# A two-layer transformer block on one core: 32 stored copies of a distance table in place of 128, and each later bias load split in four

## The reference

```python
d_own = pos[:, None] - (own * MOBA_BLOCK + blk_off)[None, :]
s_own = jnp.einsum('bhqd,bhkd->bhqk', qc, k_own) * scale
s_own = jnp.where(d_own >= 0, s_own + rel_table[:, rel_bucket(d_own)].astype(jnp.float32)[None], NEG)
p = jax.nn.softmax(logits, axis=-1)          # logits = s_own here
```

## Time and profile before

| | us |
|---|---|
| median of 3 runs | 2872.69 |
| lowest, highest of them | 2869.83, 2874.22 |
| the profiled execution, its own time | 2870.79 |
| its span (first to last instruction) | 2869.1 |

### The profile page before, as it was taken

One profiled execution on the slowest core, in us unless ns is written; L12 is line 12 of the kernel. 1 busy time (PEld: TensorE's weight loads), 2 busy tenths in 40 slices (PEclk: granted clock), 3 DMA queues, 4 the chain that ended last, 5 costly groups with the idle time before them and its releaser, 6 DMA issues.

```text
span 2869.1 us, 58709 instructions
## 1 busy us (share of the span) xinstructions
PE 2811.4 (98%) x22998; PEld 2767.3 (96%) x22998; DVE 1651.9 (58%) x2115; ACT 1251.6 (44%) x1531; POOL 114.2 (4%) x133
## 2 busy tenths in 40 slices
PE   7999999999999999999999999999999999999998
PEld 7888899999999999999999999999999999999998
DVE  6455677666666544554555755555655555555444
ACT  5345555444344344443444554444544444344333
POOL 0002220000000000000001400000000000000000
PEclk9999999999999999999999999999999999999999
DMA  6543455555555655556555445555555555555555
GB/s 218 125 131 105 111 145 169 187 174 196 183 183 175 197 185 178 188 182 185 174 175 166 160 156 184 186 184 184 176 177 190 190 185 185 185 177 190 184 170 176
DMA packets 141133, 499.99 MB, mean 174 GB/s; under 512 B 17405, under 2 KB 19837, under 8 KB 141024
## 3 DMA queue, kind: packets, MB, share of 16 engines
q1 hardware_dynamic: 136912, 491.36, 52.4%
q0 software_dynamic: 4112, 7.02, 1.7%
HBM read 494.06 MB, written 4.19 MB: 174 GB/s over the span
## 4 chain that ended last, share of the span: by engine, by line
PE 91%; DVE 3%; ACT 2%; DMA 1%; issue 1%; DVEq 1%; ACTq 0%; SPq 0%
PE acc L1199 29%; PE acc L1201 29%; PE acc L1200 29%; DVE wlo L744 1%; DMA raw<-in_wts 1%; ACT whi L424 1%; PE aux L1241 1%; PE aux L1232 0%; PE aux L1306 0%; PE aux L1308 0%; DMA h<-in_hT 0%; PE aux L1300 0%; DVE h L786 0%; PE aux L1421 0%; PE aux L1314 0%
## 5 line engine op out<-in xcount | busy, mean ns | idle before, releaser
L744 DVE TENSOR_TENSOR wlo<-raw,whi 128x1024 fp32r<-128x1024 f32 x926 | 1121.4, 1230 | 863.0 <-ACT whi L424 858.7
L1199 PE MATMUL acc<-xh,whi 128*128 128x256 f32 (+2 forms) x4976 | 1419.1, 285 | 26.4 <-DVE wlo L744 16.7
L1201 PE MATMUL acc<-xh,wlo 128*128 128x256 f32 (+2 forms) x4976 | 1404.9, 282 | 0.0
L1200 PE MATMUL acc<-xl,whi 128*128 128x256 f32 (+2 forms) x4976 | 1402.0, 282 | 0.0
L424 ACT ACTIVATE whi<-raw 128x1024 fp32r<-128x1024 f32 x926 | 954.4, 1054 | 868.4 <-PE acc L1201 790.5
L1199 PEld LDWEIGHTS acc<-xh,whi 128*128 128x128 f32 x4976 | 941.8, 189 | 37.1 <-issue 19.8
L1200 PEld LDWEIGHTS acc<-xl,whi 128*128 128x128 f32 x4976 | 938.9, 189 | 0.7
L1201 PEld LDWEIGHTS acc<-xh,wlo 128*128 128x128 f32 x4976 | 939.3, 189 | 0.0
L1199 PE MATMUL acc<-acth,whi 128*128 128x256 f32 x1408 | 396.8, 282 | 4.6 <-issue 4.5
L1200 PE MATMUL acc<-actl,whi 128*128 128x256 f32 x1408 | 396.3, 281 | 0.0
L1201 PE MATMUL acc<-acth,wlo 128*128 128x256 f32 x1408 | 396.2, 281 | 0.0
(11 more groups left out here) (281 smaller groups left out, 2370.7 us busy)
## 6 DMA issues: line engine op xcount, KB each, us to landing
raw<-in_wts SPq DMA_DIRECT2D x928, 512.0 KB, 4.3
h<-in_hT SPq DMA_DIRECT2D x4, 544.0 KB, 4.8
distances<-quads POOLq DMA_DIRECT2D x1, 2048.0 KB, 47.8
bias<-distances POOLq DMA_DIRECT2D x16, 128.0 KB, 2.4
out_T<-h SPq DMA_DIRECT2D x4, 512.0 KB, 3.5
bias<-in_rp POOLq DMA_DIRECT2D x16, 64.0 KB, 4.9
bias<-in_rp POOLq DMA_DIRECT2D x8, 44.0 KB, 4.6
bias<-in_rp POOLq DMA_DIRECT2D x8, 42.0 KB, 4.6
```

What stands on the lines that cost most here:

```text
L744: dve.tensor_tensor(wlo[:, slot_of(at, j), :], raw[:, slot_of(at, j), :], whi[:, slot_of(at, j), :].bitcast(F32), ALU.subtract).then_inc(l ...
L1199: pe.matmul(dst, hi, x_hi(kt), start=kt == 0, stop=False)
L1200: pe.matmul(dst, hi, x_lo(kt), start=False, stop=False)
L1201: last = pe.matmul(dst, lo, x_hi(kt), start=False, stop=kt == chunks * per_chunk - 1)
```

## The change

The stored table has 32 copies in place of 128. Row p of a group of 32 partitions reads copy p, and each 128-partition load becomes four loads of 32 partitions, whose start in the table is moved back by the group's first partition. DVE waits for the larger count of landed loads. The bias that arrives is the same.

```diff
+COPIES = 32
...
-    dist_dram = nc.dram_tensor("distances", (P, HEADS, DISTS + 1), F32, kind="Internal").ap()
+    dist_dram = nc.dram_tensor("distances", (COPIES, HEADS, DISTS + 1), F32, kind="Internal").ap()
...
+        MOBA_LOADS = 2 * (P // COPIES) * 16
...
-            pool.dma_start(dist_dram.rearrange("c h d -> h c d"), dist.unsqueeze(1).to_broadcast([HEADS, P, DISTS + 1]))\
+            pool.dma_start(dist_dram.rearrange("c h d -> h c d"), dist.unsqueeze(1).to_broadcast([HEADS, COPIES, DISTS + 1]))\
...
-                    pool.dma_start(bias2[:, t, :],
-                                   bass.AP(dist_dram.tensor, i * (DISTS + 1) + (SEQ - 1 - t * P),
-                                           [[HEADS * (DISTS + 1) - 1, P], [1, SEQ]])).then_inc(bias_landed, 16)
+                    for p in range(0, P, COPIES):
+                        pool.dma_start(bias2[p:p + COPIES, t, :],
+                                       bass.AP(dist_dram.tensor, i * (DISTS + 1) + (SEQ - 1 - t * P - p),
+                                               [[HEADS * (DISTS + 1) - 1, COPIES], [1, SEQ]])).then_inc(bias_landed, 16)
...
-                        scaled_scores(MOBA, i, bias2, (bias_landed, i * 32 + (16 * NA_DMAS * HEADS + 32)))
+                        scaled_scores(MOBA, i, bias2, (bias_landed, i * MOBA_LOADS + (16 * NA_DMAS * HEADS + MOBA_LOADS)))
```

## The result

| | before | after |
|---|---|---|
| median, us | 2872.44 (6 runs) | 2858.59 (6 runs) |
| lowest to highest | 2869.83 to 2874.22 | 2854.95 to 2860.08 |
| profiled execution's span | 2869.1 | 2858.4 |

The ratio is 0.995, with an interval of 0.994 to 0.996: 13.9 us faster by the medians. The two profiled executions differ by only 10.7 us.

A forecast was written before the change was run, and what follows sets the result against it. TensorE, busy 98% of the span, was taken as the bound, waiting only where the store delayed weight loads. 2870.79 - 14.69 = 2856.1 us, or 2858.0 by the runs' median; 2857.0 was predicted, half-way, range 2853.5 to 2865.

The forecast's parts named there:

- The store goes with its bytes: Table store on GpSimd's queue: a quarter of the bytes takes a quarter of 47.8 us, 12.0, ending near 113.7.
- The first weight load is in time: MLA head 0: the load issued behind the store at 104.53 lands by 117.0, before ScalarE rounds it near 117.9.
- The cover up to 121.9: MLA head 0: rounding the first chunk as late as 121.9 us costs TensorE nothing; the upper bound was 120.3.
- The whole excess goes, 14.69 us: MLA heads 0 and 1 fall from 68.21 us to twice undisturbed head 2, 53.52; everything behind moves forward 14.69 us.
- the forecast that the wait for `qkv` would be gone: MLA heads 0 and 1: a sign of success was that TensorE's waits for `pt` and `qkv` would be gone.
- The mask and the first NA bias earlier: GpSimd's mask load, small loads and addition move to about 115 to 126 us; price 0 to 1.95 us, taken as nothing.
- The eight loads: MOBA heads: eight bias loads for two, 4.5 us of GpSimd per head, hidden; cost nothing, upper bound 2 us.
- The rival of latency: Queue alternation, not backlog, delays the first load: only head 1 recovers, 7.3 us left, 2863.5 or 2865.4; chance 7%.
- The rival that the store was not the cause: The store is not the cause or its time does not follow its bytes: time stays 2870.8 to 2872.7; chance 4%.
- The Trainium skill's price: GpSimd DMA costs about 2.0 us plus bytes by 436 GB/s: store 6.8 us old, 3.2 new, so no gain, 2870.8.
- The rival of the serial loads: MOBA heads: eight small loads land one after another and slower than before; at 4.3 us each, about 2930; chance 3%.

The follow-up runs named there:

- copies64: Changed kernel with 64 copies stored and each bias load split in two: 2863.72 us, ratio 0.997 to the kernel before.
- two_copies: Kernel before with 2 copies stored, bias loads whole, rows read one element apart (wrong bias): 2857.26 us, ratio 0.995.
- split_only: 128 copies stored as in the kernel before, bias loads split in four as in the changed kernel: 2870.66 us against 2872.06, ratio 0.9999.
- store96: Kernel before with 96 copies stored, bias loads whole (wrong bias): one run, 2868.18 us.
- store_only: Kernel before with 32 copies stored, bias loads whole (wrong bias): 2859.98 us against 2872.06, ratio 0.9956.
- part128: Kernel before with its 2048 KB store read from 128 partitions of `h`, one 16 KB row each (wrong table): 2860.44 us, ratio 0.996.
- copies8: Changed kernel with 8 copies stored and each bias load split in sixteen, 32 loads a MOBA head: 2859.76 us, ratio 0.9963.

## Why the prediction was right

2857.0 was forecast, 2858.59 measured, and 13.85 us gained of 14.69. The forecast lay half-way between two sums, 2856.1 and 2858.0; the second, on the scale of the medians, is the nearer. Step by step:

- *The store goes with its bytes*, forecast 12.0 us: 12.5. Right, and the four points from 12.5 to 47.8 are nearly proportional.
- *The first weight load is in time*, forecast by 117.0: issued at 104.30, no load took over 10.9, so by 115.2. Right. The median of the loads there is 4.5 us, where I wrote near 3.5.
- *The cover up to 121.9.* Borne out by copies64: a rounding at 124.70 is late, and TensorE waits 4.1 us for `pt`. It comes 23.49 us into the head, against 23.87 before, where the wait was 4.5, so each us beyond the cover costs about one.
- *The whole excess goes, 14.69 us.* The mechanism is right, the term was too large by 0.8. "Heads 0 to 2 have the same six chunks and the same attention steps" was not like with like. A group of eight chunks ends in head 1 at step 1 (`j % CD == CD - 1` for j = 7), and TensorE waits there 1.5 us for the eviction, also when the store is nearly nothing (two_copies). That this boundary is the reason is read from the order of the program. Undisturbed, heads 0 and 1 take 26.21 + 28.09 = 54.30 and not 2 x 26.76 = 53.52. For the same reason the forecast that the wait for `qkv` would be gone was wrong: 3.9 of its 5.4 us went.
- *The mask and the first NA bias earlier.* The addition runs from 125.48 to 127.42, as forecast. Its cost, taken as nothing, shows in heads 0 and 1 only as one instruction (L840) of 0.70 us. The 1.3 us that this profile lost in the later NA heads lie within the spread of all profiles.
- *The eight loads.* 3.9 us of GpSimd in place of the 4.5 forecast, hidden in a head of 25.16 us; nothing lost (split_only).
- *The rival of latency.* Half right as a mechanism: a weight load is let in after 22 us even if the store goes on (store96). It did not decide, because a store of 12.5 us ends before.
- *The rival that the store was not the cause* fell with store_only and split_only. The Trainium skill's price in DMA: Bandwidth & Descriptors (Anatomy of one DMA), an estimate of 6.8 us for 2 MB, agrees with part128's 7.5; for 8 source partitions the measured 47.8 decides. The page's advice (Rules for kernel authors) to put a dimension whose size is a multiple of 16 outermost, so that all 16 DMA engines are used, agrees with the traces: 50.8% of the engines at 8 and 100.4% at 16. It is not enough, since from 16 to 128 partitions the time still falls by three, 22.9 to 7.5.
- *The rival of the serial loads* was wrong: in copies8 a load lands after a median of 2.8 us, so 32 of them one after the other would need 90 us, and a head stays at 25.16. The loads overlap. What ends the cover is GpSimd's issue pitch of 0.58 us, with which 32 loads a head fit and 64 do not.

## What to carry to other kernels

A store that nobody waits for can still hold up the loads that everybody waits for: read the time to landing of each DMA against its bytes, and where it is far above its neighbours, look at what was issued while it was out. Spread the source over many partitions first, and cut its bytes if that cannot be done. When the excess of a disturbed stretch is taken from an undisturbed one, check that group boundaries fall in the same steps in both.

## What the runs showed of the hardware that I had not expected

- A store from 8 partitions runs at 6.1 GB/s for each, from 16 at 5.7: 43.1, 22.9 and 7.5 us for 2 MB from 8, 16 and 128 partitions. The first keeps half of the 16 DMA engines busy, the other two all.
- Beside the 8-partition store, a 512 KB load waits up to 22 us and then comes at one in 6.3 us when the store's rows are 2 KB, and waits 39 us when they are 16 KB (one profile).
- VectorE instructions that meet a GpSimd tensor addition of 1.94 us are stretched until 0.3 us behind its end, as one from 0.41 to 2.04 us.
- After an idle time of 2.2 to 3.0 us TensorE's clock fell in ten of fourteen profiles and stayed in four; the length of the idle time does not tell which (2.37 to 2.90 us where it stayed, 2.24 to 3.00 where it fell). The fall cost 1 to 4 us.
